# Narrower moving operands in the pair products of a two-block transformer kernel's decay attention

## What is computed

```
b = jnp.cumsum(lfb, axis=2)                        # log decay, per head and channel
diff = b[:, :, :, None, :] - b[:, :, None, :, :]
decay = jnp.exp(jnp.where(mask[:, :, None], diff, -jnp.inf))
att = jnp.einsum('bhtd,bhsd,bhtsd->bhts', qb, kb, decay)
o = jnp.einsum('bhts,bhse->bhte', att, vb) + ...   # and the state of earlier chunks
```

## Time and profile before

| | |
|---|---|
| median of 3 runs | 2521.74 us (2521.15 to 2523.29) |
| the profiled execution | 2523.29 us |
| its span, first to last instruction | 2521.5 us |
| mean granted TensorE clock | 0.959 |
| TensorE matmul busy | 2330.7 us (92%) |
| VectorE / ScalarE busy | 1597.1 us (63%) / 1116.2 us (44%) |

### The profile page before, as it was taken

The page is one execution under the profiler, slowest core; times in us unless marked ns, Lnnn a source line. Parts: engine busy times, 40 slices in busy tenths (PEclk is TensorE's granted clock), DMA queues, the critical chain, the costliest instruction groups (busy, mean ns, idle before and its releaser), DMA issues.

```text
span 2521.5 us, 41119 instructions
## 1 busy us (share of the span) xinstructions
PE 2330.7 (92%) x17410; PEld 2121.9 (84%) x17410; DVE 1597.1 (63%) x2601; ACT 1116.2 (44%) x1751; POOL 127.5 (5%) x130
## 2 busy tenths in 40 slices
PE   6998997999978999998998988998998998988997
PEld 3665686999867998988998978997668998987997
DVE  3376455554876655687556686655987656687555
ACT  3424335334345344744435445334555334745333
POOL 0011100000000000000000000002740000000000
PEclk9998998999989999998999989999999999998999
DMA  7245533554223554413554414553014554512551
GB/s 312 85 164 215 222 116 120 187 183 165 84 78 139 184 184 152 180 54 134 187 191 139 153 51 151 184 185 116 1 68 151 184 186 149 185 66 97 188 184 68
DMA packets 50296, 368.33 MB, mean 146 GB/s; under 512 B 5568, under 2 KB 5696, under 8 KB 5824
## 3 DMA queue, kind: packets, MB, share of 16 engines
q1 hardware_dynamic: 49968, 363.59, 39.9%
q10 hardware_dynamic: 144, 2.10, 0.2%
HBM read 364.62 MB, written 1.05 MB: 145 GB/s over the span
## 4 chain that ended last, share of the span: by engine, by line
PE 78%; DVE 14%; ACT 4%; issue 2%; DMA 1%; SPq 0%; DVEq 0%; ACTq 0%
PE psum L225 64%; DVE weight_parts L219 2%; PE psum L3680 1%; DMA weight_ring<-stream_dram 1%; PE psum L3681 1%; PE psum L2524 1%; DVE work L989 1%; PE psum L3009 1%; PE psum L407 1%; ACT weight_parts L193 1%; PE psum L552 1%; DVE work L984 1%; PE psum L1629 1%; DVE work L2833 1%; PE psum L3698 1%
## 5 line engine op out<-in xcount | busy, mean ns | idle before, releaser
L225 PE MATMUL psum<-input_parts,weight_parts 128*128 128x256 f32 x8448 | 1031.7, 285 | 47.6 <-DVE input_parts L997 27.0
L225 PEld LDWEIGHTS psum<-input_parts,weight_parts 128*128 128x128 f32 x8448 | 1024.8, 193 | 56.6 <-issue 50.8
L219 DVE TENSOR_TENSOR weight_parts<-weight_ring,weight_parts 128x1024 fp32r<-128x1024 f32 x536 | 631.9, 1220 | 274.6 <-ACT weight_parts L193 273.6
L193 ACT ACTIVATE weight_parts<-weight_ring 128x1024 fp32r<-128x1024 f32 x540 | 541.3, 1051 | 265.9 <-PE psum L225 265.1
L225 PE MATMUL psum<-hidden_parts,weight_parts 128*128 128x256 f32 x3936 | 481.1, 283 | 11.1 <-DVE hidden_parts L2650 6.6
L225 PEld LDWEIGHTS psum<-hidden_parts,weight_parts 128*128 128x128 f32 x3936 | 473.6, 190 | 16.3 <-issue 8.8
L1071 ACT ACTIVATE work<-psum 128x256 f32<-128x256 f32 x132 | 50.6, 383 | 422.1 <-PE psum L225 422.1
L1078 DVE TENSOR_TENSOR work<-work,psum 128x256 f32<-128x256 f32 x132 | 55.6, 421 | 282.3 <-ACT work L1071 282.3
L225 PE MATMUL psum<-work,weight_ring 128*128 128x256 f32 (+1 forms) x608 | 175.7, 448 | 3.5 <-ACT work L544 2.2
L225 PEld LDWEIGHTS psum<-work,weight_ring 128*128 128x128 f32 x608 | 118.3, 196 | 56.6 <-issue 43.1
L225 PE MATMUL psum<-weight_ring,silu_cond 128*32 128x256 f32 x768 | 56.5, 416 | 18.3 <-DMA weight_ring<-stream_dram 18.3
(11 more groups left out here) (465 smaller groups left out, 2369.4 us busy)
## 6 DMA issues: line engine op xcount, KB each, us to landing
weight_ring<-stream_dram SPq DMA_DIRECT2D x341, 1024.0 KB, 4.8
constants<-constants_dram SPq DMA_DIRECT2D x1, 2176.0 KB, 14.0
work<-s_bc_dram ACTq DMA_DIRECT2D x1, 2048.0 KB, 8.1
work<-ctx_dram SPq DMA_DIRECT2D x1, 1024.0 KB, 7.8
residual<-x_dram SPq DMA_DIRECT2D x1, 1024.0 KB, 9.8
out_dram<-residual SPq DMA_DIRECT2D x1, 1024.0 KB, 3.9
vectors<-vectors_dram SPq DMA_DIRECT2D x1, 550.5 KB, 3.7
constants<-constants_dram SPq DMA_DIRECT2D x1, 65.0 KB, 3.5
```

The lines of the kernel that those rows point to most:

```text
L193: act.activation(self.parts[:, s % SPLITS, 0, cols], self.ring[:, i % RING, cols], ACT.Identity)\
L219: ins = dve.tensor_tensor(self.parts[:, s % SPLITS, 1, cols], self.ring[:, i % RING, cols], self.parts[:, s % SPLITS, 0, cols].bitcast(F32 ...
L225: mm = pe.matmul(*args, **kw)
```

## The change

The view `later` is dropped. The moving operand is taken from the tile itself, and always has its own 64 later columns; the bank receives 64 columns per call. Stationary operand, number and order of calls, banks and signals are the same.

```diff
--- before.py
+++ after.py
@@ -2992,7 +2992,6 @@
             mm.then_inc(job.full[0], 1)
         for l, b in enumerate(H_LEVELS):
             e = src.pairs[l % 5].rearrange("p (h t) -> p h t", h=HEADS)
-            later = halves(src.pairs[l % 5], b)[:, :, 1, :]
             pe.wait_ge(*src.e_ready[l])
             for j, job in enumerate(self.jobs[l]):
                 begin(pe, job)
@@ -3004,10 +3003,9 @@
                     for t in range(2):
                         cols = slice(t * P, (t + 1) * P)
                         at = (2 * i + t) * P // 2
-                        width = min(P, BANK - at)
-                        first = (2 * h + t) * P // (2 * b)
-                        mm = pe.matmul(job.ap[:, at:at + width], (e if b > 1 else kk)[:, h, cols],
-                                       later[:, first:first + width // b, :], start=True, stop=True)
+                        right = e[:, h, cols].rearrange("p (m s b) -> p m s b", s=2, b=b)[:, :, 1, :]
+                        mm = pe.matmul(job.ap[:, at:at + P // 2], (e if b > 1 else kk)[:, h, cols], right,
+                                       start=True, stop=True)
                 mm.then_inc(job.full[0], 1)
         v = src.v
         pe.wait_ge(*src.v_ready[-1])
```

## The result

The changed kernel takes 2547.3 us (median of 4 runs, 2541.9 to 2552.4) where the kernel before takes 2521.4 (4 runs): a ratio of 1.0094, with a 95% interval of 1.0074 to 1.0115, which is +18.7 to +29.0 us. Executions of one kernel spread by more than the 0.1% given ahead: 27 of the kernel before reach from 2508.8 to 2530.4 us (median 2522.6), and all 15 of the changed kernel from 2533.4 to 2552.4 (median 2543.5).

A forecast was written before the change was run, and what follows sets the result against it. TensorE, busy 92% of the span, was taken to bound the kernel, with L3009's last levels on the path. Low clock until the readout adds 9.8 us (layer 0) and 12.0 (layer 1): 21.8 on 2521.7 gives 2543.5; range 2527 to 2557.

The forecast's parts named there:

- The pace: L3009's narrowed matmuls at full clock: the weight load sets the step, about 0.113 us, so 64 columns give back 0 to 0.4 us.
- Rival B: L3009's step follows the columns, about 0.056 us, until VectorE's copies set the end: 2520.3 us; chance 0.05.
- The low step: L3009's records at 1.2 GHz: width does not matter there either, and each record takes 0.213 us.
- The fall: Clock drop to 1.2 GHz in L3009's levels, no later than before: +7.3 to +9.0 us layer 0, +9.0 to +10.6 layer 1.
- No return: Half-empty 64-column steps do not bring 2.4 GHz back before the readout in either layer; all 21.8 us hang on it.
- The return in the readout: The readout begins at low clock and its 256- and 512-column matmuls bring the clock back, at 1.6 us a layer.
- Carried through whole: After L3009, copies, readout and next projection form a chain without transfer waits, so the whole delay, 21.8 us, reaches the end.
- A: Rival: the clock follows how busy TensorE is, which stays as busy, so 2521.7 us within 0 to 0.4; chance 0.15.
- C: Rival: low clock from the first narrow level of L3009, without a wait, +34.7 us, 2556 us; chance 0.05.
- D: Rival: low clock holds in one layer only, or returns for a level in between: +6 to +16 us; chance 0.09.

## Why the prediction was right

The forecast was 2543.5 us and +21.8; the median of four is 2547.3 (of all fifteen 2543.5), and the two stages lost 23.1. With the spread of whole times, how near the median comes to the forecast is in part luck; the stages are the test. Two rows of the kernel before are needed below: weight loads of 64 rows and 64 columns of another stage, and L3009 just behind its low stretch in layer 0.

```profile
319.50 1.35 PEld L2102 LDWEIGHTS psum<-work,spare 64*64 64x64 f32 x22
...
1108.70:1117.00 8.30, 8.30 (x75) 8.20 (x73) 1.00 0.01 2
```

- **The pace.** Forecast: no gain from 64 columns, 0.114 us as before. Measured: the same 10.83 us for the first 96 records. Rival B is out. That the weight load is what the step is paid for was argued from the 2-column rows; a row of the kernel before bears it out, where loads of 64 rows and 64 columns step by (1.35 - 0.135) / 21 = 0.058 us at clock 1.00, with 64 moving columns as in the changed call (rows and columns of the load shrink together there, so it does not tell which of them sets the step). The Trainium skill ("TensorE: Matmul & The Clock Gate", LDWEIGHTS) gives a load of P columns P/1.2 ns, 107 ns for 128 by an estimate. That is near the 0.113 us measured at full clock; at low clock the step is 0.214. The formula of the Trainium skill for the gap between matmuls ("TensorE: Matmul & The Clock Gate", Back-to-back issue gap), N/2.4 + 2.5 ns, which the prediction took for rival B, does not fit the step here. The Trainium skill gives it there for an isolated matmul and says that it counts too little at small N, where each has its own weight load; the prediction left that out.
- **The low step.** Forecast 0.213 us a record. Measured from start to start, 128 records took 26.88 us, 0.210 each, with the first few still at full clock. The last 64 of the run with 2-column calls, all at low clock, took 13.69 us (1106.79 to 1120.48), 0.214 each.
- **The fall.** Forecast between the level b = 8 and today's place in layer 0, and from b = 16 at the earliest in layer 1. It came within b = 8 in layer 0 (0.6 us behind 1089.83) and within b = 16 in layer 1 (0.7 us behind 2253.57), each behind the wait in front of that level, at the early end of both ranges. Before the readout this cost +8.6 against 7.3 to 9.0, and +10.0 against 9.0 to 10.6. That it fell inside the range in layer 1 is in part luck: with the same first four levels it fell in b = 32 in the run with the last three wide, earlier than the prediction held possible.
- **No return.** This was the step on which most hung. It held in both layers, and the run with the last three levels narrow, the one with them wide and the one with 2-column calls bear it out. The earlier trace rows have no row for the other half of the argument, that 128-column records bring the clock back; the second row above does: 1.00 from 1108.7, behind 0.50 up to 1108.5.
- **The return in the readout.** Mis-sized: 1.6 us was taken from a level of 128-column records, and it cost 2.2 and 2.35. The low clock lasts through six calls of the readout in layer 0, until 1121, and seven in layer 1, and these take twice as long. It came back under the 256- and 128-column calls, ahead of the first one of 512 columns (1121.54), so it did not need those as the prediction had it. This is the 1.3 us between 21.8 and 23.1; before the readout the two layers lost 18.6, as forecast.
- **Carried through whole.** It held within the stages. "Spans outside the two stretches unchanged to within a us" did not: the line begins 8.8 us earlier in the profiled execution of the changed kernel, and 8.1 us later in layer 1, and layer 0's loss explains 10.8 of these 16.8.
- **The rivals.** A (the clock follows how busy the engine is) had 0.15. Taken by the busy records it was refuted twice: by 17.86 busy us of 18.2 in front of a fall, and by 48.90 of 48.90 without a return, both with 2-column calls. C (low from the first narrow level) is out in both layers. D did not occur.

Why TensorE's clock treats half-empty steps so is not shown by any run. Shown is the comparison: with the same narrow records and equally filled waits, the clock held with 256- and 512-column calls and fell with 2-column ones.

## What to carry to other kernels

Before narrowing a matmul, read the step from one record to the next: where it is set by the weight load, fewer moving columns give next to nothing back, and the columns that are dropped may be what keeps the clock up. Compare the granted clock and the step, not the busy share; it was 93% here against 92% before. Where a stage alternates short matmul bursts with waits, a few wide calls into an unused bank inside the waits hold the clock, which pays only where TensorE sets the end of what follows.

## What the runs showed that was not expected

The dense projections, which no edit touches, do not have one pace. Records of L225 in two stretches of 50 us, first in the kernel before, then in the changed one (length, busy with count of PE and PEld, clock, DMA):

```profile
460.00:510.00 50.00, 50.00 (x419) 50.00 (x418) 1.00 0.49 174
1240.00:1290.00 50.00, 50.00 (x429) 50.00 (x428) 1.00 0.51 184
```

```profile
460.00:510.00 50.00, 50.00 (x429) 50.00 (x428) 1.00 0.51 188
1240.00:1290.00 50.00, 50.00 (x424) 50.00 (x423) 1.00 0.51 187
```

TensorE is busy throughout, at full clock, and gets through 419 or 429 records in the one stretch and 429 or 424 in the other. Each profiled execution has its own combination: the same 417 records behind 450 us of the kernel before took 50.04, 49.48 or 48.93 us over the eight traces, and the same 426 behind 1200 us took 49.98 to 51.12 us, in steps of about 0.56. Records missing from a trace are not the reason, since all eight have the same 17410 matmul records beside the extra ones. Much of the drift between two executions outside the stages builds up in these projections. Another part comes from the clock in stages that no edit touches: from the first record of L3363 (L3361 in the changed kernel) to the next projection, 1436.62 to 1489.45 before and 1439.40 to 1495.53 after, 52.8 and 56.1 us pass, at a mean clock of 0.68 and 0.63. Both are probably why the times of one kernel spread over 20 us; that was not tested. What chooses the pace was not tried.
